# Hybrid decoder layer on one core: x's first quarter on another DMA queue, two sums of x moved behind four products, one item's scores in two parts

## The reference

```python
x = x + 0.5 * swiglu(rmsnorm(x, norm_ffn1), ffn1_w_in, ffn1_w_out)      # swiglu: (silu(u) * v) @ w_out, d_ff = 2816
x = x + hybrid_mixer(rmsnorm(x, norm_mix), ...)
x = x + 0.5 * swiglu(rmsnorm(x, norm_ffn2), ffn2_w_in, ffn2_w_out)
out = rmsnorm(x, norm_final)
```

```python
s = jnp.einsum('bqghd,bngd->bghqn', qc, kc) * scale
p_c, _, _ = masked_softmax_stats(s, cmp_end[None, :] <= t[:, None])
o_c = jnp.einsum('bghqn,bngd->bqghd', p_c.astype(vc.dtype), vc)
```

## Time and profile before

| | us |
|---|---|
| median of 3 runs | 1142.19 (1141.85 to 1143.57) |
| profiled execution, its own time | 1144.03 |
| its span, first to last instruction | 1142.2 |
| PE busy | 1123.4 |
| DVE busy | 788.8 |
| ACT busy | 517.7 |
| mean granted clock of PE | 0.997 |

### The profile page before, as it was taken

How to read it: one execution, slowest core, us unless ns; L and a number is a source line. 1 busy time by engine, 2 the same in 40 slices (tenths; PEclk the granted TensorE clock), 3 DMA queues, 4 the chain that set the end, 5 groups by cost and what they waited for, 6 DMA issues and landing times.

```text
span 1142.2 us, 16722 instructions
## 1 busy us (share of the span) xinstructions
PE 1123.4 (98%) x6799; PEld 925.1 (81%) x6799; DVE 788.8 (69%) x1110; ACT 517.7 (45%) x757; POOL 137.0 (12%) x174
## 2 busy tenths in 40 slices
PE   8999999999999999999999999999999999999997
PEld 6778888888888987877778888888887888888885
DVE  7985888679955466566676344555795789459845
ACT  6642564245534233443445523356742565146533
POOL 1000000000010472346771000000000000000000
PEclk9999999999999999999999999999999999999999
DMA  8051326113514631413132232522052226204401
GB/s 305 24 203 37 111 74 221 37 43 106 184 47 122 153 84 43 96 54 82 45 83 50 75 101 80 181 90 101 10 184 74 74 74 221 74 8 141 147 1 74
DMA packets 111548, 111.78 MB, mean 98 GB/s; under 512 B 30896, under 2 KB 76384, under 8 KB 111472
## 3 DMA queue, kind: packets, MB, share of 16 engines
q1 hardware_dynamic: 106912, 104.97, 29.0%
q0 software_dynamic: 4400, 5.61, 1.8%
q10 hardware_dynamic: 160, 0.14, 0.0%
HBM read 105.71 MB, written 2.10 MB: 94 GB/s over the span
## 4 chain that ended last, share of the span: by engine, by line
PE 90%; DVE 7%; ACT 1%; issue 1%; DMA 0%; SPq 0%; DVEq 0%; ACTq 0%
PE ps L1994 11%; PE ps L1996 11%; PE ps L1995 11%; PE ps L1844 9%; PE ps L1845 8%; PE ps L1846 8%; PE ps L2010 6%; PE ps L2011 6%; PE ps L2012 6%; PE ps L1912 2%; PE ps L2128 2%; PE ps L2172 1%; PE ps L2201 1%; DVE w_lo L1500 1%; DVE probs L1458 1%
## 5 line engine op out<-in xcount | busy, mean ns | idle before, releaser
L1500 DVE TENSOR_TENSOR w_lo<-raw,w_hi 128x1024 fp32r<-128x1024 f32 (+1 forms) x124 | 142.0, 1185 | 65.0 <-ACT w_hi L1007 64.9
L1007 ACT ACTIVATE w_hi<-raw 128x1024 fp32r<-128x1024 f32 (+1 forms) x124 | 121.0, 1024 | 115.3 <-PE ps L2012 108.2
L2010 PE MATMUL ps<-w_hi,pu_hi 128*128 128x512 f32 x352 | 138.3, 393 | 0.1
L2012 PE MATMUL ps<-w_hi,pu_lo 128*128 128x512 f32 x352 | 137.1, 389 | 0.0
L2011 PE MATMUL ps<-w_lo,pu_hi 128*128 128x512 f32 x352 | 137.1, 389 | 0.0
L1994 PE MATMUL ps<-w_hi,xg_hi 128*128 128x512 f32 x320 | 125.3, 392 | 1.5 <-DVE square L1604 1.5
L1995 PE MATMUL ps<-w_lo,xg_hi 128*128 128x512 f32 x320 | 124.6, 389 | 0.0
L1996 PE MATMUL ps<-w_hi,xg_lo 128*128 128x512 f32 x320 | 124.5, 389 | 0.0
L1270 DVE TENSOR_TENSOR w_lo<-w_raw,w_hi 128x1024 fp32r<-128x1024 f32 (+4 forms) x42 | 75.3, 1793 | 54.6 <-ACT w_hi L890 54.6
L1844 PE MATMUL ps<-xg_hi,w_hi 128*128 128x512 f32 x272 | 108.5, 399 | 0.0
L1846 PE MATMUL ps<-xg_hi,w_lo 128*128 128x512 f32 x272 | 106.1, 390 | 0.0
(11 more groups left out here) (287 smaller groups left out, 2155.9 us busy)
## 6 DMA issues: line engine op xcount, KB each, us to landing
raw<-in_ffn_w_in SPq DMA_DIRECT2D x20, 1024.0 KB, 4.9
w_raw<-in_ffn_w_in SPq DMA_DIRECT2D x20, 1024.0 KB, 5.0
w_raw<-in_w_in SPq DMA_DIRECT2D x32, 512.0 KB, 4.3
raw<-in_ffn_w_out SPq DMA_DIRECT2D x14, 1024.0 KB, 5.9
w_raw<-in_ffn_w_out SPq DMA_DIRECT2D x6, 1024.0 KB, 4.9
w_raw<-in_w_in SPq DMA_DIRECT2D x24, 256.0 KB, 3.9
raw<-in_ffn_w_in SPq DMA_DIRECT2D x16, 256.0 KB, 5.7
w_raw<-in_w_out SPq DMA_DIRECT2D x8, 512.0 KB, 4.4
```

The lines of the kernel that those rows point to most:

```text
L1007: nc.scalar.activation(w_hi[:, (BASE[i] + g) % 2, part], op_raw(g)[:, part], ACT.Copy).then_inc(up_sems["op_hi"], 1)
L1500: V.tensor_tensor(w_lo[:, sl, part], op_raw(g)[:, part], w_hi[:, sl, part].bitcast(F32), ALU.subtract).then_inc(up_sems["op_lo"], 1)
L2010: mm(bank, ph, wh, start=(k == 0 and start), stop=False)
L2012: last = mm(bank, pl, wh, start=False, stop=(stop and k == nk - 1))
```

## The change

x's part 0 is asked for by ACT's queue, ahead of the gains and constants; SP's queue no longer asks for it. In ffn1 alone (i == 0) DVE forms S2 and S4 after the four products of the plain part, and ACT takes their high parts in unit 1 behind operand 3 and ahead of the negated block. The compressed scores are issued in two parts: masks and query tiles 0 and 1, then the values step of the pair's first item (n = 2), then query tiles 2 and 3, then the values step of n = 3.

```diff
+        def load_x(eng, part, m0, m1, n):
+
+            xv = x[0].rearrange("(t p) d -> p t d", p=P)
+            for tt in range(0, TT, n):
+                eng.dma_start(x_nat[:, tt:tt + n, m0 * P:m1 * P], xv[:, tt:tt + n, m0 * P:m1 * P]).then_inc(x_landed[part], 16)
...
         @block.sync
         def _(sp):
-            xv = x[0].rearrange("(t p) d -> p t d", p=P)
-
-            def load_x(part, m0, m1, n):
-                for tt in range(0, TT, n):
-                    sp.dma_start(x_nat[:, tt:tt + n, m0 * P:m1 * P], xv[:, tt:tt + n, m0 * P:m1 * P]).then_inc(
-                        x_landed[part], 16)
-
             load_pair(sp, 0, 0, ffn1_w_in)
-            load_x(0, 0, 2, 2)
             load_pair(sp, 0, 1, ffn1_w_in)
-            load_x(1, 2, 4, 2)
+            load_x(sp, 1, 2, 4, 2)
             load_pair(sp, 0, 2, ffn1_w_in)
-            load_x(2, 4, KD, 1)
+            load_x(sp, 2, 4, KD, 1)
...
-            act_sum(act, i, S4)
-            act_sum(act, i, S2)
+            if i:
+                act_sum(act, i, S4)
+                act_sum(act, i, S2)
             act.wait_ge(rstd_ready, 2 * i + 1)
...
             act_op(act, i, g0 + 1)
+            if u == 1 and i == 0:
+                act_sum(act, i, S4)
+                act_sum(act, i, S2)
             act_minus(act, i, u)
...
         @block.scalar
         def _(act):
+            load_x(act, 0, 0, 2, 2)
             act.dma_start(vec_rows[0:KD, :], norm_ffn1[0].rearrange("(m p) -> m p", p=P)).then_inc(gain_landed, 16)
...
-            for o in (S1, S2, S4):
+            for o in (S1, S2, S4) if i else (S1,):
                 dve_sum(dve, i, o)
...
+            if i == 0:
+                dve_sum(dve, i, S2)
+                dve_sum(dve, i, S4)
...
-        def pe_scores(pe, n):
+        def pe_scores(pe, n, part=0):
             it, b = ITEMS[n], 2 * (n % 2)
-            if n >= 2:
+            if n >= 2 and part == 0:
                 pe.wait_ge(pt_act, n - 1)
             if it[0] == "cmp":
-                for g in range(2):
+                for g in range(2 if part == 0 else 0):
...
-                for qt in range(TT):
+                for qt in range(2 * part, 2 * part + 2):
...
-                last.then_inc(scores_psum, 1)
+                if part:
+                    last.then_inc(scores_psum, 1)
                 return
...
                 for nn in (n, n + 1):
                     if nn < b - 1:
                         pe_values(pe, nn)
+                    if nn == n and n + 3 < b and ITEMS[n + 3][0] == "cmp":
+                        pe_scores(pe, n + 3, 1)
```

## The result

The changed kernel takes 1146.6 us (median of 6 runs, 1145.87 to 1147.77) against 1142.22 for the kernel before in the same session (6 runs): ratio 1.0038, 95% interval [1.0025, 1.0051]. It is 4.4 us slower, where 1.2 was forecast, and outside the range given. Its profiled execution took 1146.52, its span 1144.7.

The account below looks back on a forecast made before the run. PE, busy for 98% of the span, was taken to bound the kernel. The terms 0 + 1.06 + 0.13 = +1.2 us, added to the median of 1142.19, gave 1143.4 us, range 1141.4 to 1145.1.

Parts of the forecast that it names:

- the term of part 1: Kernel start, x's first quarter on ACT's queue: first product stays near 8.97 us, so 0, bounds -1.0 and +0.6.
- the even share: Kernel start: ACT's and SP's queues share the engines evenly, so the constants end near 6.6 us.
- The 0.5 from the end of the bytes to PE: Kernel start: PE sees the constants 0.5 us after their last byte, near 7.1 us.
- The bound of +0.6: Kernel start, upper bound for x's move: constants seen 1.2 us after their last byte.
- 1.0 us earlier: Kernel start: x's two DMAs, asked for at 0.74 instead of 1.75 us, come 1.0 us earlier.
- The rival of the clock: Scores' fill or the new wait at 40.4 us: clock falls in most runs, 1145.1 for the former; chance 0.2.
- Part 2: ffn1, S2 and S4 behind the products: DVE loses time waiting at the gains' copy, +1.06 us, bounds -1.47 and +2.1.
- Part 3: Compressed scores in two parts: PE's stop for instructions stays, 152 records left behind it, +0.13 us, bounds -1.65 and +0.73.
- the rival by which the stop belongs to the run of small scores: Compressed scores: the stop breaks up when a values step parts the run, 1141.6 us; chance 0.12.
- a fall in the scores' fill: Compressed scores: a clock fall there costs 1.7 us; the median of the timed runs was taken to be without it.

Follow-up runs that it names:

- The two experiments on order: Against the kernel before: x's quarter on ACT's queue behind gains and constants, 1145.96 us; on SP's queue ahead of the first weight pair, 1143.6 us.
- The experiment with the fill: Only the sums moved against the kernel before, with S2 formed while DVE waits for the gains' transpose: 1142.1 us, ratio 0.9997.
- part 2 alone: Only the sums S2 and S4 moved behind the products, against the kernel before: 1143.62 us, ratio 1.0006.
- x first on SP's queue: The kernel before with x's first quarter asked for ahead of the first weight pair, still on SP's queue: 1143.6 us, ratio 1.0012.
- part 3 alone: Only the compressed scores issued in two parts, against the kernel before: 1143.56 us, ratio 1.0002.
- three orders tried: x's quarter, against the kernel before: on ACT's queue ahead of gains and constants 1144.63 us, behind them 1145.96; on SP's ahead of the weights 1143.6.

## Why the prediction was wrong

**The failed step is the term of part 1**: "so they end near 6.6 and are seen 0.5 later, near 7.1", "I take 0", with +0.6 as its upper bound. It measured +2.0 alone and +2.6 in the whole. Three things went wrong in it.

*The constants' share.* The bytes were right: 1.15 MB had moved by 6 us and 1.9 by 8, and the two queues shared evenly as long as x's quarter was on ACT's. But I carried the even share on to the constants. They got 18% in the stretch from 6 to 8, ended near 8.1 and not 6.6, and were seen at 8.1 to 8.8 in four profiles. The 0.5 from the end of the bytes to PE held (0.4). What made the share fall stays open; x's larger load kept near a half on the same queue in the same stretch. The bound of +0.6 held the time from the last byte to PE to be the only uncertainty, not the share itself, though no row showed two full queues, as the prediction said.

*What the lead was worth.* The prediction let x be "1.0 us earlier" by its issue time. The two experiments on order show that bytes, not issues, set this start: a quarter of x ahead of the weights made them 2.6 us late, and on the second queue it took 8.2 us from asking to use where it had taken 5.7, as I read it because SP's later loads, not needed yet, came in between. The page "DMA: Bandwidth & Descriptors" of the Trainium skill (Issuing engines are not separate DMA queues) had it so: only issue time is saved. The runs agree and go further, as even that was not saved on the way to the first product. The prediction quoted the page and still left more room for a gain (1.0) than for a loss (0.6).

*The clock at the start.* The clock's fall was weighed at 40.4 and at the scores, and not at the one wait that part 1 made longer. PE's idle time between the warm-ups and the constants grew from none to 2.1 to 2.8, and the fall that came in it or within 1 us of its end costs 1.3 to 2.0 by the profiles and 1.4 by the timed runs. The rival of the clock had the right mechanism, and its total of 1145.1 was nearer than the forecast; its place was wrong. In none of the three profiles of the whole change did the clock fall at 42 or in the scores.

**Part 2 was right** in mechanism and size: the wait at 34 gone, 1.26 of DVE's time lost, 1.8 at the chain copy, 0.5 at the turned half, +1.01 for +1.06 in the trace (the timed +1.0 alone doesn't exclude no change). The experiment with the fill shows its cause.

**Part 3 was right** in the count: 192 became 180, and warm-ups added 440 us earlier made 186 out of 192 and 178 out of 180. That rules out the rival by which the stop belongs to the run of small scores. The size is right too, once it is taken from where PE goes on after the stop: from there to the transposes it is 8.07 before and 8.16 to 8.18 in all five profiles with the scores in parts, +0.1 for a term of +0.13. What made it look like -0.2 to +0.3 from the masks on is the end of the stop, which comes 4.4 to 5.0 after the masks from one execution to another, whichever the kernel. The instruction queue moved one packet between 447.6 and 448.2 in the profile before and none from there until PE went on at 450.38, which fits a PE that waits for a block; the fetch itself was not varied. The page "Runtime: NRT & Kernel Launch" of the Trainium skill (Instruction fetch mechanics) says the fetch is hidden; the trace disagrees here, where 256 instructions last 1.2 us and a block takes 3.7 to come (446.7 to 450.38 before).

What the prediction had wrong at this place is the clock. It took the median to be without the fall of the earlier trace rows, and a fall in the scores' fill to cost 1.7. But all nine profiles in which the scores are in one run have a stretch at half there. In six it came before the transposes (from 449.9 to 455.8), where PE waits anyway, and cost nothing when it lasted 3.41 us and about 0.5 when it lasted 6.83; only behind the transposes (before, part 2 alone, x first on SP's queue, and part 3 alone) did it cost 1.3 to 2.0 (683.4 to 683.8 to the end of the span, against 681.8 to 682.1). Of the five profiles with the scores in parts four have none. So the change may spare some executions this fall; what that is worth in the timed runs no comparison here shows.

**Sum by the runs**: 2.6 for part 1 (1.3 late and 1.4 clock, each rounded), 1.4 for parts 2 and 3: 4.0 in that session, 4.4 in the first.

## What to carry to other kernels

At a start that waits for bytes, a load asked for earlier, on its own queue or on another, delayed what shared the engines with it in each of the three orders tried; list what the first product needs in bytes, and move nothing that isn't needed ahead of it or between. An operation moved out of a busy engine's queue gains only what that engine doesn't then spend waiting, so look first for work to put into that wait, and for work ahead of the next release that is needed later. And a lengthened wait of PE has two prices, itself and the clock behind it: price both at every place, the first one too.

## What the hardware showed that was not expected

- The small load (130 KB) behind two full queues got 18% of the moved bytes, where the large one before it had got near a half, and x's load, in the same stretch of the kernel that had it behind the constants, 0.28 of 0.62 MB.
- Idle times of PE and the clock, one profile each. Near 48 us it fell within an idle time of 3.00 us, for 6.83 us; pieces of 1.8 and 0.5 left it alone. At the start, idle times of 1.2 and 1.35 were followed by no fall; 2.1 and 3.02 by one of 3.41 us, 0.9 and 1.2 us after their end; in those of 2.8 and 3.69 it fell for 6.83 us.
- At the scores the same kind of wait had different outcomes: PE's idle time of 2.2 ahead of the transposes was followed by 3.41 us at half in one profile and by none in four. The place of a fall matters more than its length: 6.83 us at half where PE had to wait anyway cost about 0.5, 3.41 us behind the transposes 1.3 to 2.0.
- PE's stop for instructions moves with the count of all instructions issued before it: three more warm-up matmuls in the first 10 us moved a stop at 450 us by exactly their six records.
